# Two seven-product feed-forward stages: first-column products moved into the units in front, a new order of products, tiles and joins

## The chip, the core and the metric

The kernel runs on one core of a Trainium2 chip. The metric is the device time of one execution in microseconds. TensorE is PE in the profile, its weight loads PEld, VectorE DVE, ScalarE ACT, GpSimd POOL and SyncE SP; SP issues the DMA transfers of the stages that matter here.

## What is computed

Two transformer blocks on x of 1024 tokens by 1024 columns, all in float32. The two places that the change touches are the first halves of the two feed-forward layers, here called block 1's and block 2's up stage:

```python
h = rmsnorm(x, g_ffn[i])
x = x + jnp.square(jax.nn.relu(h @ w_ffn_up[i])) @ w_ffn_down[i]      # block 1: 1024 x 4096, 4096 x 1024
...
up = depthwise_conv(h @ w_up[l], conv_f_w[l], conv_f_b[l], FFN_CONV // 2)   # block 2: 1024 x 5632, three taps
act = jax.nn.gelu(up[..., :D_FF_2], approximate=True) * up[..., D_FF_2:]
x = x + act @ w_down[l]                                                # 2816 x 1024
```

## The kernel before

**Products.** A float32 matmul is three matmuls (`three`, L398 to L402): each operand is kept as a high part, rounded, and a low part, the rest. For a weight tile ACT writes the high part (`weight_hi`, L435) and POOL the low part behind it (`weight_lo`, L457). PE can start on the tile when both are there.

**Units.** An up stage goes in units of 256 output columns: 16 in block 1 (f=1), 22 in block 2 (f=2). A unit's weights are two column blocks, the activations two token halves by two column halves, and the four quarter results are made with seven products in place of eight. Each product is twelve matmuls of 128x512 (4 column pieces by three). In the order of before:

- P1 and P2 use the first-column tile, called F here, a plain weight tile `weight_hi<-stage` of 128x1024. P1 writes a PSUM bank, ACT copies it to `kept` (L2266), and P2 adds onto the same bank, so P2 waits for that copy.
- P6 and P7 use tile A (`sum23`), P5 and P4 tile B (half `sum1`, half plain), P3 tile C (`sum4`, 128x512). The sums are four DVE instructions of 128x512 for a unit (`dve_weight_sums`, L486 to L491).
- Joins on DVE: U2 = P6 + kept (L2291), U3 = P7 + kept (L2294), and an output from each of P5, P4 and P3 (L2307). P7 waits for U2, P4 for U3, P3 for P5's join, because they add onto or reuse those banks.
- Block 1 then does relu and square on ACT (L2273 to L2279) and stores the result. Block 2 runs the three taps: `act_conv` (ACT, L2167) and two DVE instructions of 128x1024 (L2175, L2176), then gelu (ACT, L2183) and the product with the other half (DVE, L2190).

The activations' quarters (T1, T2, T3, T4, B22 and so on) are split too: `T_hi` by ACT (L724), `T_lo` by DVE (L736) or by POOL (L744).

**The weight ring.** In these stages four weight slots go round. Step `released` in the order, behind the last product of a tile, frees the tile's slot and puts the split of the tile four further on in that place of ACT's, POOL's and (for sums) DVE's queue. Every engine works its queue in order. `P2`, `P7`, `P4` and `P3` are the last products of F, A, B and C:

```python
def released(self, n=1):
    for _ in range(n):
        self.back += 1
        s = self.slot_of[self.back - 1]
        ...
            self.slot(s)
```

**The seam.** At the start of a stage the norm of the token rows 4 to 7 still runs while PE works on P1 of the units 0 to 3 (EARLY = 4), then on their P2; then the units begin, each unit from the fifth on with its own P1 and P2 inside: P1, P6, P2, P7, P5, P4, P3. At the end the down stage takes over: it needs split activations (`act_hi`, `act_lo`, L2373 and L2382) and weight tiles of its own.

Of the kernel before, what the change touches and what calls it, by code (L numbers as in the profile page):

```python
# [14 lines left out]
P = 128  # L15
S = 1024
# [40 lines left out]
OUTS, EARLY = 4, 4  # L57
SUM_ROWS, LATE_ROWS, RAW_ROWS = (0, 1, 2), (3, 4), (6, 7)
SPILLED = {1: SUM_ROWS + LATE_ROWS, 2: SUM_ROWS + LATE_ROWS + RAW_ROWS}
# [666 lines left out]

def dve_split_lo(K, nid, name, t):
    if name not in LOW_BY_POOL:
# [10 lines left out]
def pool_split_lo(K, nid, name, t):  # L739
    if name in LOW_BY_POOL:  # L740
        g, S = K.g, K.S
        (hi, lo), raw = quarter(K, name, t)
        g.wait_ge(S.hT_hi, (nid, name, t))
        g.q.tensor_tensor(lo, raw, hi.bitcast(F32), ALU.subtract).then_inc(*S.hT_lo_pool.up((nid, name, t)))  # L744


LOW_BY_POOL = ("T4",)


def need_quarter(K, nid, name):  # L750
    t = NT // 2 - 1 if name in ("B11", "B21") else NT - 1
    K.pe.wait_ge(K.S.hT_hi, (nid, name, t))
    K.pe.wait_ge(K.S.hT_lo_pool if name in LOW_BY_POOL else K.S.hT_lo, (nid, name, t))

# [1401 lines left out]
def act_conv(K, u, part):  # L2156
# [87 lines left out]
def out_slot(u, name):  # L2244
    return u if name == "P2" and u < EARLY else OUTPUTS[name][0]


def out_before(u, name):

    if name == "P2" and u < EARLY:  # L2250
        return None
    if u == 0:
        return OUTPUTS[name][0], "P2"
    if name == "P2" and u == EARLY:
        return None
    return u - 1, name


def act_product(K, f, u, name):
# [22 lines left out]
def dve_product(K, f, u, name):  # L2282
# [29 lines left out]
def sp_product(K, f, u, name):  # L2312
# [18 lines left out]
def sp_x_back(K, f, t):  # L2331
# [9 lines left out]
    elif t in LATE_ROWS:  # L2341
        sp.wait_ge(S.mm, ("P4", f, last))
    else:
# [533 lines left out]
def lay_out(K):  # L2877
# [112 lines left out]
    K.kept = [put("kept", [P, HALF]) for _ in range(KEPT_ROWS)]  # L2990
# [133 lines left out]
class Order:  # L3124
# [30 lines left out]
    def take_unit(self, f, u, first, second, again):  # L3155

        w = len(self.tiles)
        if again:
            r1 = self.load(first, ("sums", (f, u)), w)
        else:  # L3160
            r1 = self.load_of[self.unit_tiles[f, u][0]][0]
            self.load_uses[r1].append(("sums", (f, u)))
            self.load_end[r1] = w
        r2 = self.load(second, ("sums", (f, u)), w)
        self.load_uses[r2].append(("low", w + 1))
        self.load_end[r2] = w + 1
        for part in (2, 3, 4):
            self.load_of.append((r1, r2))
            self.tiles.append((None, (P, 4 if part == 4 else ND, P)))
            self.sums_of.append((f, u, part))  # L3170
        self.unit_tiles[f, u] += (w, w + 1, w + 2)
# [421 lines left out]

def order_unit_up(o, f, norm):

    io, units = o.io, UNITS_UP[f]
# [476 lines left out]
```

## Time and profile before

| | |
|---|---|
| three runs | 3518.33, 3519.07, 3520.52 us (median 3519.07) |
| the profiled execution | 3518.79 us, its span 3517.5 us |
| granted clock of PE, mean | 0.984 of full speed |
| PE, PEld busy | 96%, 78% of the span |
| DVE, ACT, POOL busy | 57%, 40%, 36% |
| block 1's up stage in the trace | about 1187 to 1518 us |
| block 2's up stage in the trace | about 2788 to 3282 us |

The span is the stretch that the trace covers; 1.3 us of the profiled execution lie outside it. A window's row gives for each engine its busy time and in brackets how many instructions began there. A PE instruction's busy time overlaps that of the next one, so time lost on PE is better read from the distance between starts than from idle time alone.

### The profile page before, as it was taken

What the parts mean: (1) busy time and instruction counts of PE and PEld (TensorE: products, weight loads), DVE (VectorE), ACT (ScalarE), POOL (GpSimd) and SP (SyncE); (2) the same over time, 40 slices, a digit from 0 to 9 for tenths busy, and PEclk for the clock granted to TensorE, in tenths of its full rate; (3) what the DMA queues carried; (4) which work ended last, traced back from release to release, by engine and by line L of the source; (5) the groups of instructions that cost most, each with busy time, mean ns of one, the idle gap of its engine ahead of it and who ended that gap; (6) DMA issues with size and microseconds to landing.
All of it is one profiled execution on the core that took longest, in us unless ns stands there. A gap on an engine that the chain in (4) does not pass through costs nothing.

```text
span 3517.5 us, 48865 instructions
## 1 busy us (share of the span) xinstructions
PE 3371.2 (96%) x19926; PEld 2730.7 (78%) x19926; DVE 2012.0 (57%) x2693; ACT 1395.0 (40%) x2361; POOL 1268.9 (36%) x694
## 2 busy tenths in 40 slices
PE   7999999999999899999999899999999969999999
PEld 6788888887668778888887677777788757777787
DVE  3655747337754733345555539985554666666554
ACT  4443433344433544431114547771232424444212
POOL 3212122110033434454441126662453335555542
PEclk9999999999999999999999999999999989999999
DMA  5101101110046233342222322223565312222422
GB/s 153 40 24 44 48 25 46 41 45 7 1 147 206 90 105 109 108 170 96 96 96 96 109 68 81 81 81 106 177 205 176 102 60 79 83 78 102 144 101 85
DMA packets 312015, 326.57 MB, mean 93 GB/s; under 512 B 14117, under 2 KB 232673, under 8 KB 311792
## 3 DMA queue, kind: packets, MB, share of 16 engines
q1 hardware_dynamic: 297184, 289.17, 25.4%
q10 hardware_dynamic: 11520, 25.17, 1.9%
q0 software_dynamic: 3088, 9.10, 0.7%
q8 instruction: 159, 2.61, 0.3%
q14 instruction: 64, 0.52, 0.0%
HBM read 252.08 MB, written 71.30 MB: 92 GB/s over the span
## 4 chain that ended last, share of the span: by engine, by line


## 5 line engine op out<-in xcount | busy, mean ns | idle before, releaser
L457 POOL TENSOR_TENSOR weight_lo<-stage,weight_hi 128x1024 fp32r<-128x1024 f32 (+4 forms) x269 | 615.4, 2293 | 1094.9 <-ACT weight_hi L435 1066.4
L2432 DVE TENSOR_TENSOR x<-x,psum 128x512 f32<-128x512 f32 x416 | 283.4, 687 | 281.5 <-PE psum L402 265.2
L435 ACT ACTIVATE weight_hi<-stage 128x1024 fp32r<-128x1024 f32 (+4 forms) x329 | 299.9, 925 | 327.1 <-PE psum L402 282.8
L400 PE MATMUL psum<-hT_hi,weight_hi 128*128 128x512 f32 x1024 | 411.4, 402 | 3.7 <-ACT weight_hi L435 2.1
L401 PE MATMUL psum<-hT_lo,weight_hi 128*128 128x512 f32 x1024 | 401.0, 392 | 0.0
L402 PE MATMUL psum<-hT_hi,weight_lo 128*128 128x512 f32 x1024 | 400.8, 391 | 0.0
L400 PE MATMUL psum<-weight_hi,act_hi 128*128 128x512 f32 x864 | 337.8, 391 | 4.7 <-DVE raw L2307 3.3
L401 PE MATMUL psum<-weight_lo,act_hi 128*128 128x512 f32 x864 | 337.3, 390 | 0.0
L402 PE MATMUL psum<-weight_hi,act_lo 128*128 128x512 f32 x864 | 337.1, 390 | 0.0
L457 POOL TENSOR_TENSOR weight_lo<-sum,weight_hi 128x512 fp32r<-128x512 f32 (+1 forms) x114 | 209.7, 1848 | 212.0 <-ACT weight_hi L435 212.0
L400 PE MATMUL psum<-T_hi,weight_hi 128*128 128x512 f32 x608 | 244.6, 402 | 38.7 <-DVE U L2291 32.1
L401 PE MATMUL psum<-T_lo,weight_hi 128*128 128x512 f32 x608 | 242.7, 399 | 0.0
L402 PE MATMUL psum<-T_hi,weight_lo 128*128 128x512 f32 x608 | 242.3, 399 | 0.0
L400 PEld LDWEIGHTS psum<-hT_hi,weight_hi 128*128 128x128 f32 x1024 | 193.7, 189 | 53.7 <-issue 5.5
L401 PEld LDWEIGHTS psum<-hT_lo,weight_hi 128*128 128x128 f32 x1024 | 193.9, 189 | 42.9 <-issue 4.1
L402 PEld LDWEIGHTS psum<-hT_hi,weight_lo 128*128 128x128 f32 x1024 | 193.6, 189 | 41.2
L400 PEld LDWEIGHTS psum<-weight_hi,act_hi 128*128 128x128 f32 x864 | 162.9, 189 | 39.8 <-DVE raw L2307 3.7
L400 PE MATMUL psum<-B_hi,weight_hi 128*128 128x512 f32 x456 | 180.7, 396 | 9.2 <-ACT kept L2266 6.6
L402 PEld LDWEIGHTS psum<-weight_hi,act_lo 128*128 128x128 f32 x864 | 162.9, 189 | 33.9
L401 PEld LDWEIGHTS psum<-weight_lo,act_hi 128*128 128x128 f32 x864 | 162.9, 189 | 33.6
L2382 POOL TENSOR_TENSOR act_lo<-act_raw,act_hi 128x1024 fp32r<-128x1024 f32 x54 | 128.9, 2408 | 147.7 <-ACT act_hi L2373 147.7
L435 ACT ACTIVATE weight_hi<-sum 128x512 fp32r<-128x512 f32 (+1 forms) x114 | 87.8, 771 | 235.4 <-DVE sum L491 178.5
(416 smaller groups left out, 7164.6 us busy)
## 6 DMA issues: line engine op xcount, KB each, us to landing
stage<-in_w_in SPq DMA_DIRECT2D x64, 512.0 KB, 3.8
act_raw<-scratch_act SPq DMA_DIRECT2D x54, 512.0 KB, 5.2
stage<-in_w_up SPq DMA_DIRECT2D x48, 512.0 KB, 3.7
stage<-in_w_ffn_up SPq DMA_DIRECT2D x36, 512.0 KB, 4.1
scratch_gates<-gate ACTq DMA_DIRECT2D x64, 256.0 KB, 2.0
gs<-scratch_gates SPq DMA_DIRECT2D x64, 256.0 KB, 2.9
stage<-in_w_out SPq DMA_DIRECT2D x32, 512.0 KB, 4.5
scratch_act<-out SPq DMA_DIRECT2D x64, 256.0 KB, 2.5
```

The source lines that it names most:

```text
L400: q.matmul(out, stat[0], mov[0], start=first, stop=False, skip_group_check=onto)
L401: q.matmul(out, stat[0], mov[1], start=False, stop=False, skip_group_check=onto)
L402: return q.matmul(out, stat[1], mov[0], start=False, stop=final, skip_group_check=onto)
L435: a.q.activation(hi[:, part], src, ACT.Copy).then_inc(*S.w_hi.up(w))
L457: g.q.tensor_tensor(lo[:, part], src, hi[:, part].bitcast(F32), ALU.subtract).then_inc(*S.w_lo_pool.up(w))
L2382: g.q.tensor_tensor(lo, K.act_raw[i % 4][:, :], hi.bitcast(F32), ALU.subtract).then_inc(*S.act_lo.up((f, i)))
L2432: v.q.tensor_tensor(dst, dst, K.bank(key), ALU.add).then_inc(*S.x.up(("f", f, g, t, n)))
```

## The change

- P1 and P2 of the units 5 and up ("singles") no longer stand in their own unit. `unit_products` deals them out over the units in front, one behind P7 and the rest behind P3. In some units two are placed, in some one.
- A unit's own products go P6, P5, P7, P4, P3.
- Five units (EARLY = 5) have P1 and P2 in the seam. The fifth `kept` buffer lies in the place of row 5 of x, which is therefore stored away and brought back; the rows of the down stage are ordered anew.
- Tiles are taken in the order in which they are released; the first column block is loaded a second time for the sums of every unit, which adds 28 transfers of 512 KB (11 units in block 1, 17 in block 2).
- Joins stand apart from their products: those of P7 and P5 behind P7, taps begin with `conv_first` ahead of the join or the split.
- In the seam ten high splits of quarters stand behind P1 of unit 0 instead of two, and B22's low split for rows 4 and 5 goes to POOL.
- PSUM's ring of banks starts at bank 0 at the first down product.

```diff
-OUTS, EARLY = 4, 4
+OUTS, EARLY = 4, 5
 SUM_ROWS, LATE_ROWS, RAW_ROWS = (0, 1, 2), (3, 4), (6, 7)
-SPILLED = {1: SUM_ROWS + LATE_ROWS, 2: SUM_ROWS + LATE_ROWS + RAW_ROWS}
+KEPT_ROW = 5
+SPILLED = {1: SUM_ROWS + LATE_ROWS + (KEPT_ROW,), 2: SUM_ROWS + LATE_ROWS + (KEPT_ROW,) + RAW_ROWS}
...
+def low_by_pool(name, t):
+    return name == "T4" or (name == "B22" and t in POOL_LOW_ROWS)
...
+        elif u == KEPT_ROWS - 1:
+            a.wait_ge(S.spill[KEPT_ROW], f)
+            a.wait_ge(S.xn, (K.up_norm[f], KEPT_ROW))
...
-FIRST_ROWS = {1: (5, 6, 7, 0, 1, 2, 3, 4), 2: (5, 0, 1, 2, 3, 4, 6, 7)}
+FIRST_ROWS = {1: (6, 7, 0, 1, 2, 3, 4, 5), 2: (0, 1, 2, 3, 4, 5, 6, 7)}
...
+    if (g, t, n) == (0, FIRST_ROWS[f][0], 0):
+        K.ring_at["all"] = 0
...
+    def take_first(self, f, u, first):
+        self.unit_tiles[f, u] = (self.take(first),)
+
+    def take_part(self, f, u, part, first, second):
 
         w = len(self.tiles)
-        if again:
+        if part == 2:
...
+RELEASES = {"P2": 1, "P7": 2, "P4": 3, "P3": 4}
+
+
+def unit_products(f):
+
+    units = UNITS_UP[f]
+    singles = [(v, name) for v in range(EARLY, units) for name in ("P1", "P2")]
+    plan, done = [], 0
+    for u in range(units):
+        upto = min(len(singles), -(-u * len(singles) // (units - 2)))
+        more = singles[done:upto]
+        done = upto
+        plan.append([(u, "P6"), (u, "P5"), (u, "P7"), *more[:1], (u, "P4"), (u, "P3"), *more[1:]])
+    return plan
...
-    def block(u, i):
-        return weight_block(up, unit_blocks(f, u)[i] * P)
-
-    def first(u):
-        o.unit_tiles[f, u] = (o.take(block(u, 0)),)
-
-    def rest(u, again):
-        o.take_unit(f, u, block(u, 0), block(u, 1), again)
-    nid = {1: 2, 2: 5}[f]
-    for u in range(EARLY):
-        first(u)
-    for u in range(EARLY):
-        rest(u, True)
-    for u in range(EARLY, units):
-        first(u)
-        rest(u, False)
-
-    def product(u, name, back=1):
+    plan = unit_products(f)
+    early = [(u, name) for us in (range(EARLY - 1), range(EARLY - 1, EARLY)) for name in ("P1", "P2") for u in us]
+    for u, name in early + [p for unit in plan for p in unit]:
+        if name in RELEASES:
+            blocks = [weight_block(up, i * P) for i in unit_blocks(f, u)]
+            if name == "P2":
+                o.take_first(f, u, blocks[0])
+            else:
+                o.take_part(f, u, RELEASES[name], *blocks)
+
+    def product(u, name, join=True, back=True):
         o.do("product", f, u, name)
-        if name in ("P2", "P7", "P4", "P3"):
-            o.released(back)
+        if join:
+            o.do("join", f, u, name)
+        if back and name in RELEASES:
+            o.released()
...
     advance(norm, 2)
-    o.do("spill", f, LATE_ROWS[1])
-    if f == 2:
-        for t in RAW_ROWS:
-            o.do("spill", f, t)
+    for t in (LATE_ROWS[1], KEPT_ROW) + (RAW_ROWS if f == 2 else ()):
+        o.do("spill", f, t)
     product(0, "P1")
     advance(norm, 1)
-    high("T2", 4, 5)
+    for name in ("T2", "T4", "B22", "T1", "T3"):
+        high(name, 4, 5)
+    for name in ("T4", "B22"):
+        low(name, 4, 5)
     low("T2", 4, 5)
     o.released()
     product(1, "P1")
     advance(norm, 1)
-    high("T3", 4, 5)
-    low("T3", 4, 5)
+    low("T1", 4, 5)
     product(2, "P1")
     advance(norm, 1)
     finish(norm)
     if f == 2:
         o.do("raw_edges")
-    high("T2", 6, 7)
-    high("T3", 6, 7)
-    high("T4", 4, 5, 6, 7)
-    low("T4", 4, 5, 6, 7)
+    for name in ("T2", "T1", "T4", "T3", "B22"):
+        high(name, 6, 7)
+    low("T4", 6, 7)
     product(3, "P1")
     product(0, "P2")
     low("T2", 6, 7)
-    low("T3", 6, 7)
     product(1, "P2")
-    high("T1", 4, 5, 6, 7)
-    low("T1", 4, 5, 6, 7)
+    low("T1", 6, 7)
+    low("T3", 4, 5, 6, 7)
     product(2, "P2")
-    high("B22", 4, 5, 6, 7)
-    product(3, "P2", 0)
-    for u in range(units):
-        end = u == units - 1
-        for name in ("P1", "P6", "P2", "P7", "P5", "P4", "P3"):
-            if u >= EARLY or name not in ("P1", "P2"):
-                product(u, name)
-            if (u, name) == (0, "P6"):
+    if f == 2:
+        o.do("raw_first", 0)
+    product(3, "P2")
+    product(4, "P1")
+    product(4, "P2", back=False)
+    for u, unit in enumerate(plan):
+        for v, name in unit:
+            if v != u:
+                product(v, name)
+            elif name == "P6":
+                product(u, "P6", join=False)
+                if f == 2 and u:
+                    o.do("conv_first", u - 1, 0)
+                o.do("join", f, u, "P6")
+                if u == 0:
+                    o.released()
+                    low("B22", 6, 7)
+                if f == 2 and u:
+                    o.do("conv", u - 1, 0)
+                if u == last:
+                    for i in range(4):
+                        o.do("act_load", f, i)
+            elif name == "P5":
+                product(u, "P5", join=False)
+            elif name == "P7":
+                product(u, "P7", join=False, back=False)
+                if f == 2 and u:
+                    o.do("raw_first", u)
+                o.do("join", f, u, "P7")
+                o.do("join", f, u, "P5")
+                if f == 2 and u:
+                    o.do("gated", u - 1)
                 o.released()
-            if (u, name) == (0, "P7"):
-                low("B22", 4, 5, 6, 7)
-            if f == 2:
-                if u and name == "P6":
-                    o.do("gated", u - 1)
-                if name == "P2":
-                    o.do("raw_first", u)
-                if name in ("P4", "P3"):
-                    o.do("conv", u, 1 if name == "P4" else 0)
-            if end and name == "P1":
-                for i in range(4):
-                    o.do("act_load", f, i)
-            if end and name == "P7":
-                for i in range(2):
-                    o.do("act_split", f, i)
-                for t in SUM_ROWS[:2]:
-                    o.do("x_back", f, t)
+                if u == last:
+                    for i in range(2):
+                        o.do("act_split", f, i)
+                    for t in SUM_ROWS[:2]:
+                        o.do("x_back", f, t)
+            elif name == "P4":
+                product(u, "P4", back=False)
+                if f == 2:
+                    o.do("conv_first", u, 1)
+                o.released()
+                if f == 2:
+                    o.do("conv", u, 1)
+            else:
+                product(u, "P3")
     if f == 2:
-        o.do("gated", units - 1)
-    for t in SUM_ROWS[2:] + LATE_ROWS:
+        o.do("conv_first", last, 0)
+        o.do("conv", last, 0)
+        o.do("gated", last)
+    for t in SUM_ROWS[2:] + LATE_ROWS + (KEPT_ROW,) + (RAW_ROWS if f == 2 else ()):
         o.do("x_back", f, t)
-    if f == 2:
-        for t in RAW_ROWS:
-            o.do("x_back", f, t)
```

What this moves is seen in the order of the instructions on each engine. In the seam of block 1 ACT splits the high part of F of unit 3 (`weight_hi_59`) behind P1 of unit 0 (`kept_213` is its copy). `T_hi_199` is T2, `T_hi_203` T4, `B_hi_202` B22, `T_hi_200` T1 and `T_hi_201` T3. ACT before:

```order
L2266 ACTIVATE kept_213<-psum 128x512 [waits mm_done]
L724 ACTIVATE T_hi_199<-T_raw_204 128x4x128 [waits quarter_sum_ready] x2
L435 ACTIVATE weight_hi_59<-stage_53 128x1024 [waits stage_load1]
L2266 ACTIVATE kept_214<-psum 128x512 [waits mm_done]
L667 ACTIVATE B_raw_206<-psum 128x4x128 [waits mm_done]
L724 ACTIVATE T_hi_201<-T_raw_207 128x4x128
L724 ACTIVATE T_hi_201<-T_raw_207 128x4x128 [waits quarter_sum_ready]
```

ACT of the changed kernel, from the same copy on:

```order
L2277 ACTIVATE kept_213<-psum 128x512 [waits mm_done]
L725 ACTIVATE T_hi_199<-T_raw_204 128x4x128 [waits quarter_sum_ready] x2
L725 ACTIVATE T_hi_203<-T_raw_205 128x4x128 [waits spill_store4,spill_store3,xn_ready]
L725 ACTIVATE T_hi_203<-T_raw_205 128x4x128 [waits quarter_sum_pool_ready]
L725 ACTIVATE B_hi_202<-B_raw_206 128x4x128 [waits hT_raw_ready] x2
L725 ACTIVATE T_hi_200<-T_raw_208 128x4x128 x2
L725 ACTIVATE T_hi_201<-T_raw_207 128x4x128
L725 ACTIVATE T_hi_201<-T_raw_207 128x4x128 [waits quarter_sum_ready]
L436 ACTIVATE weight_hi_59<-stage_53 128x1024 [waits stage_load1]
```

Eight more high splits stand ahead of `weight_hi_59`.

On PE the place where a P1 begins whose tile is new, in the units of block 1. `B_hi_190` is the activation quarter of P1, `B_hi_202` that of P3, `T_hi_201` that of P7, and the number behind `weight_hi` is the slot. PE before, in the fifth unit:

```order
L401 MATMUL psum<-B_lo_196,weight_hi_59 128x512
L402 MATMUL psum<-B_hi_202,weight_lo_60 128x512
L400 MATMUL psum<-B_hi_190,weight_hi_61 128x512 [waits w_lo_pool_ready,w_hi_ready,act_op_done]
L401 MATMUL psum<-B_lo_191,weight_hi_61 128x512
L402 MATMUL psum<-B_hi_190,weight_lo_62 128x512
```

PE of the changed kernel, in unit 3, where P1 of unit 7 follows P7:

```order
L402 MATMUL psum<-T_lo_197,weight_hi_61 128x512
L403 MATMUL psum<-T_hi_201,weight_lo_62 128x512
L401 MATMUL psum<-B_hi_190,weight_hi_61 128x512 [waits w_lo_pool_ready,w_hi_ready,act_op_done]
L402 MATMUL psum<-B_lo_191,weight_hi_61 128x512
L403 MATMUL psum<-B_hi_190,weight_lo_62 128x512
```

P1 now has the slot (61) of the product directly ahead of it, so its tile can only be split once that product has ended. Counted over both stages, between the last product on a slot and the P1 that uses the slot next there stood four products in 28 of 30 places and five in two (the first tiles of the seam are not counted). Now it is none in 6 places (3 in each block), two in 11 (4 in block 1, 7 in block 2) and three in 13. P5's tile B had five or four ahead of it and has two in 6 places.

In block 2 the queues ahead of such a split. ACT before: gelu (L2183), then F (`weight_hi_57<-stage_54`), then the raw copy (L2152), A (`weight_hi_59`), B (`weight_hi_61`):

```order
L2266 ACTIVATE kept_213<-psum 128x512 [waits mm_done]
L2183 ACTIVATE xn_186<-xn_186 128x1024 [waits dve_op_done]
L435 ACTIVATE weight_hi_57<-stage_54 128x1024 [waits mm_done,stage_load2]
L2152 ACTIVATE raw_228<-psum 128x512
L435 ACTIVATE weight_hi_59<-sum_169_217 128x1024 [waits mm_done,weight_sums_ready]
L435 ACTIVATE weight_hi_61<-sum_170_218 128x512 [waits mm_done]
L435 ACTIVATE weight_hi_61<-stage_52 128x512
```

ACT of the changed kernel in a unit with two between: raw copy, gelu, A (`weight_hi_55<-sum_170`), F (`weight_hi_57<-stage_54`), and taps:

```order
L2179 ACTIVATE xn_186<-raw_229,param_50 128x1024 [waits act2_store,act_evac_done,products_joined]
L2164 ACTIVATE raw_229<-psum 128x512 [waits dve_op_done]
L2195 ACTIVATE xn_186<-xn_186 128x1024
L436 ACTIVATE weight_hi_55<-sum_170_218 128x1024 [waits mm_done,weight_sums_ready]
L436 ACTIVATE weight_hi_57<-stage_54 128x1024 [waits mm_done,stage_load2]
L2179 ACTIVATE xn_187<-raw_230,param_50 128x1024 [waits dve_op_done,products_joined]
```

DVE of the changed kernel there: U3 (L2305), P5's join (L2318), the gated product (L2202), and the four sums for which A waits:

```order
L2305 TENSOR_TENSOR U_174_222<-psum,kept_216 128x512 [waits mm_done]
L2318 TENSOR_TENSOR raw_230<-psum,U_174_222 128x512 [waits dve_op_done,products_joined]
L2202 TENSOR_TENSOR xn_186<-xn_186,xn_187 128x1024 [waits act_op_done]
L487 TENSOR_TENSOR sum_171_219<-stage_54 128x512 [waits w_lo_pool_ready,stage_load2,stage_load1]
L489 TENSOR_TENSOR sum_170_218<-sum_171_219,stage_53 128x512 [waits weight_sums_ready]
L490 TENSOR_TENSOR sum_170_218<-stage_53,stage_54 128x512
L492 TENSOR_TENSOR sum_172_220<-stage_53,sum_170_218 128x512 [waits weight_sums_ready]
```

F, which before was split ahead of A, now stands behind A, and A behind seven DVE instructions that begin with the end of P7.

## Rows read from the trace of the kernel before

**Rows 1.** The page, busy time of each engine over the span.

```profile
PE 3371.2 (96%) x19926; PEld 2730.7 (78%) x19926; DVE 2012.0 (57%) x2693; ACT 1395.0 (40%) x2361; POOL 1268.9 (36%) x694
```

**Rows 2.** Windows, block 1: stretch, length, busy of PE, PEld, DVE, ACT, POOL; clock, DMA, GB/s.

```profile
1212.00:1276.00 64.00, 51.67 (x195) 40.32 (x194) 34.06 (x39) 28.50 (x47) 28.78 (x18) 0.89 0.37 114
1276.00:1500.00 224.00, 224.00 (x986) 184.06 (x986) 83.07 (x107) 105.05 (x165) 100.77 (x59) 1.00 0.34 108
1500.00:1518.00 18.00, 16.94 (x76) 13.73 (x75) 3.46 (x5) 10.14 (x14) 12.17 (x7) 1.00 0.83 273
```

**Rows 3.** The same windows in block 2: seam, units, hand-over.

```profile
2812.00:2912.00 100.00, 70.92 (x266) 55.80 (x266) 63.46 (x64) 33.23 (x43) 39.37 (x22) 0.85 0.21 66
2912.00:3250.00 338.00, 331.45 (x1437) 266.84 (x1436) 229.02 (x240) 140.76 (x172) 179.87 (x85) 1.00 0.25 82
3250.00:3282.00 32.00, 28.38 (x111) 22.50 (x111) 17.11 (x17) 15.06 (x15) 22.93 (x9) 0.89 0.65 240
```

**Rows 4.** Waits of PE, 1198 to 1290: us in total, times, longest.

```profile
PE psum L400 <- DVE U L2291: 7.5, 4, 2.8
PE psum L400 <- issue: 3.3, 1, 3.3
```

**Rows 5.** Waits of PE, 2799 to 2925.

```profile
PE psum L400 <- DVE U L2291: 24.5, 4, 8.9
```

**Rows 6.** Waits of PE, 2925 to 3250.

```profile
PE psum L400 <- ACT kept L2266: 6.4, 17, 0.4
```

**Rows 7.** Windows, two stretches right behind a wait of PE.

```profile
1243.00:1246.40 3.40, 3.40 (x9) 2.64 (x9) 0.00 (x0) 0.00 (x0) 1.90 (x1) 0.50 0.49 139
...
2848.60:2854.10 5.50, 5.43 (x13) 4.27 (x14) 1.24 (x2) 0.99 (x2) 0.00 (x0) 0.50 0.24 95
```

**Rows 8.** Timeline of the seam of block 1: start, us, engine, instruction, idle before.

```profile
1193.04 1.04 ACT L435 ACTIVATE weight_hi<-stage 128x1024 fp32r<-128x1024 f32 x1
...
1194.16 3.23 POOL L457 TENSOR_TENSOR weight_lo<-stage,weight_hi 128x1024 fp32r<-128x1024 f32 x1 [3.00 <-ACT weight_hi L435]
...
1198.53 0.48 PE L400 MATMUL psum<-B_hi,weight_hi 128*128 128x512 f32 x1
```

**Rows 9.** Groups by form, 1186 to 1212: busy, mean ns of one, idle before.

```profile
L724 ACT ACTIVATE T_hi<-T_raw 128x512 fp32r<-128x512 f32 x12 | 6.7, 621 | 3.8 <-DVE T_raw L695 3.8
...
L744 POOL TENSOR_TENSOR T_lo<-T_raw,T_hi 128x512 fp32r<-128x512 f32 x4 | 6.7, 1698 | 0.9 <-ACT T_hi L724 0.9
```

**Rows 10.** Groups by form, the units of block 1.

```profile
L2279 ACT ACTIVATE out<-out 128x512 f32<-128x512 f32 x44 | 27.8, 632 | 1.4
...
L457 POOL TENSOR_TENSOR weight_lo<-stage,weight_hi 128x1024 fp32r<-128x1024 f32 x11 | 26.3, 2395 | 64.8 <-ACT weight_hi L435 64.8
...
L486 DVE TENSOR_TENSOR sum<-stage 128x512 f32<-128x512 f32 x11 | 20.9, 1903 | 0.0
...
L435 ACT ACTIVATE weight_hi<-stage 128x1024 fp32r<-128x1024 f32 x11 | 11.5, 1045 | 0.0
...
L2294 DVE TENSOR_TENSOR U<-psum,kept 128x512 f32<-128x512 f32 x11 | 7.6, 692 | 51.6 <-PE psum L402 51.6
...
L491 DVE TENSOR_TENSOR sum<-stage,sum 128x512 f32<-128x512 f32 x11 | 7.5, 683 | 0.0
```

**Rows 11.** Groups by form, the units of block 2.

```profile
L2176 DVE SCALAR_TENSOR_TENSOR xn<-raw,param,xn 128x1024 f32<-128x1024 f32 x34 | 59.2, 1741 | 1.2
...
L457 POOL TENSOR_TENSOR weight_lo<-stage,weight_hi 128x512 fp32r<-128x512 f32 x17 | 38.7, 2276 | 0.0
...
L2190 DVE TENSOR_TENSOR xn<-xn,xn 128x1024 f32<-128x1024 f32 x16 | 19.6, 1225 | 8.4 <-ACT xn L2183 8.4
```

**Rows 12.** Timeline of the hand-over of block 1.

```profile
1512.33 4.75 POOL L2382 TENSOR_TENSOR act_lo<-act_raw,act_hi 128x1024 fp32r<-128x1024 f32 x2
...
1517.22 0.47 PE L400 MATMUL psum<-weight_hi,act_hi 128*128 128x512 f32 x1 [1.06 <-POOL act_lo L2382]
```

**Rows 13.** Waits of PE, the hand-over of block 2.

```profile
PE psum L400 <- DVE raw L2307: 3.3, 1, 3.3
```

More of the change, by code:

```diff
@@ L739, in pool_split_lo @@
 def pool_split_lo(K, nid, name, t):
-    if name in LOW_BY_POOL:
+    if low_by_pool(name, t):
         g, S = K.g, K.S
@@ L743, in pool_split_lo @@
         g.wait_ge(S.hT_hi, (nid, name, t))
+        if name == "B22":
+            g.wait_ge(S.part, (nid, "T3", t))
         g.q.tensor_tensor(lo, raw, hi.bitcast(F32), ALU.subtract).then_inc(*S.hT_lo_pool.up((nid, name, t)))
-LOW_BY_POOL = ("T4",)
+POOL_LOW_ROWS = (4, 5)
 def need_quarter(K, nid, name):
@@ L2153, in act_raw_first, with act_conv_first @@
     K.free(key, S.act_evac)
-def act_conv(K, u, part):
+def act_conv_first(K, u, part):
     a, S, c = K.a, K.S, part * NF2 + u
@@ L2244, in out_slot, with act_join @@
 def out_slot(u, name):
-    return u if name == "P2" and u < EARLY else OUTPUTS[name][0]
+    return u if name == "P2" and u < OUTS else OUTPUTS[name][0]
 def out_before(u, name):
[L2250 to L2259, printed above, removed]
+    if name == "P2" and u <= OUTS:
+        return None if u < OUTS else (0, name)
+    return (OUTPUTS[name][0], "P2") if u == 0 else (u - 1, name)
+def act_join(K, f, u, name):
     a, S, key = K.a, K.S, ("unit", PRODUCTS[name][0], f, u)
@@ L2309, in dve_product, with sp_join @@
             K.free(key, S.joined)
-def sp_product(K, f, u, name):
+def sp_join(K, f, u, name):
     if f == 1 and name in OUTPUTS:
@@ L2342, in sp_x_back @@
         sp.wait_ge(S.mm, ("P4", f, last))
+    elif t == KEPT_ROW:
+        sp.wait_ge(S.joined, (f, last, "C21"))
     else:
@@ L2989, in lay_out @@
     m.lo = last_slot
-    K.kept = [put("kept", [P, HALF]) for _ in range(KEPT_ROWS)]
+    K.kept = [put("kept", [P, HALF]) for _ in range(KEPT_ROWS - 1)]
+    m.lo = x_at + KEPT_ROW * D * 4
+    K.kept.append(put("kept", [P, HALF]))
     m.lo = x_at
@@ L3153, in take @@
         return len(self.tiles) - len(tiles)
-    def take_unit(self, f, u, first, second, again):
+    def take_first(self, f, u, first):
+        self.unit_tiles[f, u] = (self.take(first),)
+    def take_part(self, f, u, part, first, second):
         w = len(self.tiles)
-        if again:
+        if part == 2:
             r1 = self.load(first, ("sums", (f, u)), w)
+            r2 = self.load(second, ("sums", (f, u)), w)
         else:
[L3161 to L3171, printed above, removed]
+            r1, r2 = self.load_of[self.unit_tiles[f, u][1]]
+        if part == 3:
+            self.load_uses[r2].append(("low", w))
+            self.load_end[r2] = w
+        self.load_of.append((r1, r2))
+        self.tiles.append((None, (P, 4 if part == 4 else ND, P)))
+        self.sums_of.append((f, u, part))
+        self.unit_tiles[f, u] += (w,)
     def used_upto(self):
@@ L3965, in scalar_program @@
             "output": act_output, "branch_load": act_branch_load, "gate_sum": act_gate_sum,
-            "merge_rows": act_merge_rows, "split_hi": act_split_hi, "product": act_product,
-            "act_split": act_act_split, "raw_first": act_raw_first, "conv": act_conv, "gated": act_gated, "down_rows": act_down_rows,
+            "merge_rows": act_merge_rows, "split_hi": act_split_hi, "join": act_join,
+            "act_split": act_act_split, "raw_first": act_raw_first, "conv_first": act_conv_first, "gated": act_gated, "down_rows": act_down_rows,
             "store_rows": act_store_rows, "ple_mix": act_ple_mix, "x2_stored": act_x2_stored, "rates": act_rates,
@@ L3987, in vector_program @@
             "branch_load": dve_branch_load, "gate_sum": dve_gate_sum,
-            "merge_rows": dve_merge_rows, "parts": dve_parts, "split_lo": dve_split_lo, "product": dve_product, "raw_edges": dve_raw_edges, "conv": dve_conv, "gated": dve_gated,
+            "merge_rows": dve_merge_rows, "parts": dve_parts, "split_lo": dve_split_lo, "join": dve_join, "raw_edges": dve_raw_edges, "conv": dve_conv, "gated": dve_gated,
             "down_rows": dve_down_rows, "store_rows": dve_store_rows, "p_turn": dve_p_turn, "ple_mix": dve_ple_mix,
@@ L4014, in sync_program @@
             "pair_load": sp_pair_load, "gate_load": sp_gate_load, "branch_fetch": sp_branch_fetch,
-            "gate_sum": sp_gate_sum, "residual": sp_residual, "spill": sp_spill, "product": sp_product, "x_back": sp_x_back,
+            "gate_sum": sp_gate_sum, "residual": sp_residual, "spill": sp_spill, "join": sp_join, "x_back": sp_x_back,
             "act_load": sp_act_load, "gated": sp_gated, "store_rows": sp_store_rows, "ple_load": sp_ple_load,
```

13 lines of the change are left out of this document (9 added, 4 removed).

## Prediction

> **What bounds the kernel now.** I read the page first: PE is busy for 96% of the span [rows 1], so only time in which PE stands or runs slowly can be won. The windows then say where the two up stages lose it. In the units of block 1 PE starts 986 matmuls in 224.00 us, which is 0.2272 us a matmul and 2.73 us a product of twelve, and hardly stops [rows 2]. I take 0.2272 us as the pitch and call everything above it lost. Length less count times pitch gives, in block 1, seam 64 - 195 x 0.2272 = 19.7, hand-over 18 - 76 x 0.2272 = 0.7 [rows 2]; in block 2, seam 100 - 266 x 0.2272 = 39.6, units 338 - 1437 x 0.2272 = 11.5, hand-over 32 - 111 x 0.2272 = 6.8 [rows 3]. Together 78.3 us. That is all that the change can win.
>
> The waits of PE name the causes. In block 1's seam they are four waits for U2 and one for the low part of the first A ("issue", 3.3) [rows 4]; in block 2's, four waits for U2, the longest 8.9, since U2 stands on DVE behind sums and taps [rows 5]. In block 2's units P2 waits 17 times for the `kept` copy [rows 6]; with the pipeline refilling, that is the 11.5 above. The rest of the seams' loss is the clock. Right behind a wait of 2.4 us the granted clock is 0.50 for 3.4 us, behind one of 8.4 us for 5.5 us [rows 7], half of 2.4 GHz. A stretch of 3.4 us at half speed costs 1.7 us, the longer one 2.75. I charge 1.7 for each new wait of over 2.5 us.
>
> The Trainium skill (TensorE: Matmul & The Clock Gate, "HAM oscillation") states that gaps in a stream of matmuls put the engine back to half rate, so that each gap is paid for again. By that rule, the trace agrees: 0.50 behind both.
>
> **What the change removes.** U2 gets P5 between P6 and P7, F's copies get a product in between, and seam units no longer queue four deep behind the sums. I let all 78.3 us go.
>
> **What it adds.** Let p be the end of a P7; PE could go on with the next product at p - 0.16, since starts overlap ends.
>
> *P1 directly behind P7 on the same slot, 6 places.* The tile can't be split before p. In block 1, ACT's queue has relu and square of P5's result first, and these wait for U3 and P5's join on DVE: 0.69 each, 1.3 with their overlap. Relu and square are 0.63 each (2.6), F's high part 1.05 (3.65), its low part 2.40 (6.05) [rows 10]. With the hand-overs between engines and the overlap, P1 stands 6.4 us. Three times (6.4 + 1.7) = 24.3. In block 2 there is no relu, and gelu stands ahead but mostly before p. High part 1.05 and low part 2.40 to 3.23 [rows 8, 10] give 3.5 to 4.9; I take 4.4. Three times (4.4 + 1.7) = 18.3.
>
> *P1 with two products ahead, 11 places.* F's split stands behind A's, and A's behind the four sums. Block 1, four places: joins 1.3, sums four times 0.68, 2.7 (4.0), A's high 1.05 (5.05), A's low 2.40 (7.45), F's low 2.40 (9.85) [rows 10]; PE is there at three products, 8.0. Stall 1.85, too short for me to charge the clock: 7.4. The first sum takes 1.90 us on average in block 1 [rows 10], which would make it 3.05 with a slow stretch behind it; I keep that as the upper end, 19. Block 2, seven places: joins 1.3, gated product 1.23 (2.5) [rows 11], sums 2.7 (5.2), A's high 1.05 (6.3), then two low splits of 2.40 to 3.23 each [rows 8, 10], ready at 11.1 to 12.7 against 8.0. I take the middle, 3.9, because the taps run on DVE beside the splits: they take 1.74 us on average there and half-width low splits 2.28 [rows 11]. Seven times (3.9 + 1.7) = 39.2.
>
> The Trainium skill (GPSIMD Engine Reference, "1. Specifications") states that POOL shares its SBUF interfaces with DVE and contends with DVE instructions of two SBUF inputs, as sums and taps are. The trace agrees, 3.23 us beside DVE's splits in the seam against a mean of 2.40 [rows 8, 10]; by the rule alone each stall of these seven would be the upper end, 4.7 us.
>
> *Tiles with less room in block 2.* In three units B has two products (5.5 us) from P4's end. The C21 join and `conv_first` go first (1.9 together), one half high (0.6), two halves low of 2.28 [rows 11]: 7.1, so 1.4 to 1.6 late. Where only a P2 is placed, A is late by some 0.8, three times. Together 6.6; both may be zero.
>
> *Seam, both blocks.* F of unit 3 has eight more high splits ahead (6.7 us for twelve, so 4.5) [rows 9] and on POOL four quarter splits, 1.70 each with DVE beside [rows 9]. Its high part began at 1193.04 and its low part ended at 1197.39, its P1 began at 1198.53 [rows 8]. The high part would end at about 1198.6; POOL, from 1194.2 on, needs 5.2 to 7.0 for its four and then 2.4 to 3.2 for the tile, so 1201.8 to 1204.4 and I take 1202.6. P1 is late by 4.1 us (3.2 to 5.8): twice (4.1 + 1.7) = 11.6. P2 of unit 4 stands directly behind its P1 and waits for a copy (0.8), P4 of the first and of the last unit directly behind P7 for U3 (0.95 each): 2.7 a stage, 5.4.
>
> *Hand-overs.* In block 1 the down stage's first product needs act_lo, POOL at 2.4 a piece [rows 12]. After p come joins, relu and square (2.6), a weight's high and low (6.05) and two act_lo (10.85), and only P4 and P3 are left to cover it, to 6.0: 4.85 + 1.7 = 6.6, where the wait was 1.06 [rows 12]. In block 2 the same without relu gives 4, a slow stretch 1.7, and the old wait of 3.3 for DVE behind the taps [rows 13] stays: 9.0.
>
> *At nothing:* 28 transfers of 512 KB. DMA is busy 0.34 and 0.25 of the units' windows [rows 2, 3], and 14.7 MB over 560 us is 26 GB/s beside 82 to 108. Uncovered, one landing late would cost some 4 us. The bank reset is held by the DVE wait in any case. The spill and return of row 5 lie beside products.
>
> Sum: 24.3 + 18.3 + 7.4 + 39.2 + 6.6 + 11.6 + 5.4 + 6.6 + 9.0 = 128.4. Less 78.3 it is +50.1 on the profiled execution's 3518.8, so **3569 us**; the runs' median is 0.3 us above that execution, which changes nothing.
>
> **Rivals.**
> - *Forecast, 0.58:* as above, 3545 to 3592, since the two sizes with the widest bounds (39.2 and 7.4) move it by some 12 each way and the clock by as much.
> - *Waits short, clock kept, 0.17.* New waits stand alone between full stretches, and if none is followed by half speed the sum loses 17 x 1.7 = 28.9; with POOL undisturbed it loses 3 x 0.9 + 7 x 0.8 = 8.3, and without the 6.6 it is 84.6: 3525. For it: in block 1's units all low splits ran at 2.40 [rows 10]. Against: [rows 7].
> - *Waits long, 0.14.* First sum at 1.90, two splits at 3.23, 2.75 of clock a time: 6.4 + 2.75 and 4.9 + 2.75 three times each (50.4), 19, seven times (4.7 + 2.75) = 52.2, 6.6, twice 8.5 (17), 5.4, 18: 168.6, so 3609.
> - *Faster or no change, 0.11: the sums' chain is shorter than I read it.* Its place is DVE's queue behind P7. If F's low part ended by p + 8.0, all eleven places and the 6.6 would cost nothing, 53.2 less: 3516. From there every wait followed by full speed (10 x 1.7) brings it to 3499. For it: DVE stands 51.6 us before U3 in block 1's units [rows 10], so it has time. Against: the order on DVE puts the sums behind U3 and P5's join, and then no idle time ahead of U3 helps. It decides the sign only if it is 1.9 us shorter in block 1 and 3.1 or more in block 2.
>
> **How the numbers follow.** A measurement of this kernel can tell 0.2%, 7 us, from no change. The forecast, the short and the long case lie above that, 0.89, less a part of the short one that ends within it (0.03): slower 0.86. The last rival splits into 0.07 faster and 0.04 same, so same is 0.07. The range takes in the short case and half of the long one: 3524 to 3600; it leaves out 0.11 below and some 0.07 above.
>
> **What the profile will show.** PE's waits in both up stages name POOL's `weight_lo` (or its issue), six of 4 to 6.5 us each directly behind P7, seven of 3 to 5 in block 2, with granted clock 0.50 behind them; the waits for U2 and `kept` are gone. P1 of unit 3 in each seam begins 4 us late. The units' windows fall below 1.00 in clock. I am wrong if F's low part in those places is there when P7 or P3 ends, or if PE's waits in the units add up to less than 30 us.

## The result

The changed kernel takes 3605.31 us (median of four runs, 3603.46 to 3606.92) against 3518.7 us before; the ratio is 1.0246, with a 95% interval of 1.0228 to 1.0264. It is 86.6 us slower. The forecast of slower holds, the size does not: 50 us were forecast, and the time lies 5 us above the range.

The page after, busy time by engine, against [rows 1]:

```profile
PE 3390.8 (94%) x19926; PEld 2746.3 (76%) x19926; DVE 2023.3 (56%) x2689; ACT 1388.8 (39%) x2361; POOL 1275.9 (35%) x698
```
Windows of the changed kernel (columns as in [rows 2]): the stretch that was block 1's seam, a piece behind a wait of a unit, the units of block 2, and a piece behind another wait:

```profile
1212.00:1276.00 64.00, 62.44 (x275) 51.11 (x274) 32.71 (x38) 31.28 (x50) 30.82 (x17) 1.00 0.44 134
1294.40:1298.20 3.80, 3.80 (x9) 3.03 (x10) 0.00 (x0) 0.00 (x0) 0.00 (x0) 0.50 0.02 4
2912.00:3340.00 428.00, 363.15 (x1480) 290.74 (x1478) 267.44 (x257) 142.17 (x177) 187.73 (x91) 0.93 0.28 86
2981.60:2987.80 6.20, 6.16 (x15) 4.85 (x16) 1.58 (x2) 0.66 (x2) 4.59 (x3) 0.50 0.22 65
```
From 1212 us on the seam is full where before it was empty in many places: 275 matmuls begin in 64 us against 195 [rows 2]. (One wait of this seam lies ahead of the window and is shown below.) The loss has gone into the units, which in block 1 had none: block 2's window has 1480 starts in 428 us, and 1480 x 0.2272 is 336. The second and fourth rows are work at half speed, 9 starts in 3.8 us and 15 in 6.2 us.

The waits of PE in the units of block 1 (1290 to 1545 us), then of block 2 (2915 to 3335 us), each in us in total, times, longest:

```profile
PE psum L401 <- POOL weight_lo L458: 20.2, 6, 6.3
PE psum L401 <- ACT out L2288: 7.5, 4, 1.9
```
```profile
PE psum L401 <- POOL weight_lo L458: 60.6, 19, 7.5
PE psum L401 <- DVE U L2302: 4.1, 3, 1.5
```
In block 1's units PE waited for nothing before, in block 2's for `kept` alone [rows 6]. Now it is POOL's low split nearly everywhere. The row "ACT out" is the four places with two products between: F's low part ends there within 0.1 us of one of ACT's relus (in the first at 1323.31, the relu at 1323.35), and the profile names the later one.

The first place where P1 stands directly behind P7 in block 1 (unit 3; timeline: start, us, engine, instruction). P7 ends at 1288.05, P1 begins at 1294.34:

```profile
1288.09 0.69 DVE L2305 TENSOR_TENSOR U<-psum,kept 128x512 f32<-128x512 f32 x1 [3.30 <-PE psum L403]
1288.81 0.69 DVE L2318 TENSOR_TENSOR out<-psum,U 128x512 f32<-128x512 f32 x1
1289.54 0.63 ACT L2288 ACTIVATE out<-out 128x512 f32<-128x512 f32 x1 [4.25 <-DVE out L2318]
1290.20 0.63 ACT L2290 ACTIVATE out<-out 128x512 f32<-128x512 f32 x1
1290.73 1.04 ACT L436 ACTIVATE weight_hi<-stage 128x1024 fp32r<-128x1024 f32 x1
1291.85 2.34 POOL L458 TENSOR_TENSOR weight_lo<-stage,weight_hi 128x1024 fp32r<-128x1024 f32 x1 [4.09 <-ACT weight_hi L436]
```
Joins, relu, square, high part, low part, one behind the other, as summed in the prediction: PE stands 6.45 us beyond its pitch, 6.4 were forecast. The same place in block 2 (unit 4). P7 ends at 2941.68, P1 begins at 2949.16:

```profile
2940.27 2.38 DVE L2187 SCALAR_TENSOR_TENSOR xn<-raw,param,xn 128x1024 f32<-128x1024 f32 x1 [1.66 <-ACT xn L2179]
2942.69 1.28 DVE L2188 SCALAR_TENSOR_TENSOR xn<-raw,param,xn 128x1024 f32<-128x1024 f32 x1
...
2944.01 0.60 ACT L2164 ACTIVATE raw<-psum 128x512 f32<-128x512 f32 x1 [3.77 <-DVE xn L2188]
2944.51 1.05 ACT L2195 ACTIVATE xn<-xn 128x1024 f32<-128x1024 f32 x1
2945.45 1.05 ACT L436 ACTIVATE weight_hi<-stage 128x1024 fp32r<-128x1024 f32 x1
2946.58 2.43 POOL L458 TENSOR_TENSOR weight_lo<-stage,weight_hi 128x1024 fp32r<-128x1024 f32 x1 [5.00 <-ACT weight_hi L436]
```
Here ACT's raw copy (L2164) waits until DVE has finished the taps at 2943.97, 2.3 us after P7's end. Gelu stands behind the copy, F's high part behind gelu, and the low part ends at 2949.01. PE stands 7.6 us, not 4.4. And a place of block 2 with two products between. P7 ends at 2969.53. The P2 behind it, the last product on the slot, ends at 2972.25, then come P4 and P3, and P1 begins at 2981.64, 4.1 us late, where 3.9 were forecast:

```profile
2969.57 0.69 DVE L2305 TENSOR_TENSOR U<-psum,kept 128x512 f32<-128x512 f32 x1 [2.23 <-PE psum L403]
2970.29 0.69 DVE L2318 TENSOR_TENSOR raw<-psum,U 128x512 f32<-128x512 f32 x1
2970.90 1.21 DVE L2202 TENSOR_TENSOR xn<-xn,xn 128x1024 f32<-128x1024 f32 x1
2972.03 0.68 DVE L487 TENSOR_TENSOR sum<-stage 128x512 f32<-128x512 f32 x1
...
2973.96 0.68 DVE L492 TENSOR_TENSOR sum<-stage,sum 128x512 f32<-128x512 f32 x1
2974.68 1.06 ACT L436 ACTIVATE weight_hi<-sum 128x1024 fp32r<-128x1024 f32 x1 [5.77 <-DVE sum L492]
2975.65 1.04 ACT L436 ACTIVATE weight_hi<-stage 128x1024 fp32r<-128x1024 f32 x1
2975.82 2.40 POOL L458 TENSOR_TENSOR weight_lo<-sum,weight_hi 128x1024 fp32r<-128x1024 f32 x1 [10.89 <-ACT weight_hi L436]
2978.17 3.33 POOL L458 TENSOR_TENSOR weight_lo<-stage,weight_hi 128x1024 fp32r<-128x1024 f32 x1
...
2979.33 3.25 DVE L2188 SCALAR_TENSOR_TENSOR xn<-raw,param,xn 128x1024 f32<-128x1024 f32 x1
```
The joins and the gated product begin with P7's end, and the sums run from 2972.03 to 2974.65. Then come A's high part, F's high part, A's low part (2.40) and F's low part, which takes 3.33 us with the taps on DVE beside it, against 2.34 and 2.43 above. The tap beside it takes 3.25 us, against 1.28 at 2942.69. The Trainium skill (GPSIMD Engine Reference, "1. Specifications") has POOL and DVE share their SBUF interfaces, with contention where a DVE instruction has two SBUF inputs, as the taps have; the trace agrees, by these numbers. P1 of unit 3 in the seam of block 1 began late too, by 4.4 us beyond its pitch where 4.1 were forecast:

```profile
1204.45 0.76 PE L401 MATMUL psum<-B_hi,weight_hi 128*128 128x512 f32 x1 [4.34 <-POOL weight_lo L458]
```
The hand-over of block 2, against [rows 13]: the wait for DVE is still there, now 4.1 us at the ninth product, and one for act_lo has come.

```profile
PE psum L401 <- DVE x L2447: 4.1, 1, 4.1
PE psum L401 <- POOL act_lo L2395: 3.4, 1, 3.4
```

### The profile page after: what moved, and what is told of

Read it like the earlier page. It is cut to its first block, busy times and chain, and to the rows that moved or that the text cites. A ratio compares the mean times of both kernels' runs of the same rounds, so it can differ in the third digit from the quotient of the medians.

```text
span 3605.6 us, 48830 instructions
## 1 busy us (share of the span) xinstructions
PE 3390.8 (94%) x19926; PEld 2746.3 (76%) x19926; DVE 2023.3 (56%) x2689; ACT 1388.8 (39%) x2361; POOL 1275.9 (35%) x698
## 4 chain that ended last, share of the span: by engine, by line
## 5 line engine op out<-in xcount | busy, mean ns | idle before, releaser
L401 PE MATMUL psum<-B_hi,weight_hi 128*128 128x512 f32 x456 | 193.8, 425 | 87.9 <-POOL weight_lo L458 77.7
L401 PE MATMUL psum<-T_hi,weight_hi 128*128 128x512 f32 x608 | 239.7, 394 | 19.6 <-POOL weight_lo L458 12.2
L402 PE MATMUL psum<-B_lo,weight_hi 128*128 128x512 f32 x456 | 190.3, 417 | 0.0
L403 PE MATMUL psum<-B_hi,weight_lo 128*128 128x512 f32 x456 | 189.7, 416 | 0.0
```

The costliest lines, as they stand in the source:

```text
L401: q.matmul(out, stat[0], mov[0], start=first, stop=False, skip_group_check=onto)
L402: q.matmul(out, stat[0], mov[1], start=False, stop=False, skip_group_check=onto)
L403: return q.matmul(out, stat[1], mov[0], start=False, stop=final, skip_group_check=onto)
```

## The experiments

All of them are edits of the changed kernel, but for e5, and none leaves work out. A wait's length in the rows is idle time; the text mostly gives the distance between starts beyond the pitch, which is some 0.16 us more.

**e1: deal out pairs.** In `unit_products`:

```diff
-        upto = min(len(singles), -(-u * len(singles) // (units - 2)))
+        upto = 2 * min(units - EARLY, -(-u * (units - EARLY) // (units - 2)))
```

> The changed kernel with one thing different: P1 and P2 of a unit are dealt out as a pair, both into the same unit in front or none, so that no tile has fewer than three products between the last use of its slot and its own first use (before: none in 6 places, two in 11). Products, joins, loads, seam and hand-over are those of the changed kernel, and so are the 28 additional transfers. Theory (distance on the slot): the waits of PE for POOL's weight_lo in the units go, and with them 19.4 + 8.1 us of waits in block 1, 22.9 + 28.8 in block 2, the tile B waits of 6.5 and about 32 us of half clock: 3605 - 118 = about 3487, up to 3505 if units without a pair wait for DVE. Rival A (additional transfers or splits beside DVE are too slow, wherever a single stands): stays above 3590. Rival B (the new order P6, P5, P7 itself costs): some 3550.

3498.16 us (3495.54 to 3501.74), 107 us less than the changed kernel, and 0.9946 of the time before (0.9931 to 0.9961). What PE still waits for in block 2's units:

```profile
PE psum L401 <- DVE U L2305: 9.6, 4, 2.9
PE psum L401 <- DVE U L2302: 3.8, 3, 1.5
PE psum L401 <- ACT raw L2164: 1.3, 3, 0.5
PE psum L401 <- POOL weight_lo L458: 0.4, 1, 0.4
```
The longest wait for POOL left in the units is 0.4 us, with the same loads, the same splits and the same order within a unit. The edit also brings tile B back from two products between to three or more. Rival A is out, and rival B too. What has come up are waits for U2 and U3 in the units that have no pair: there P6, P5, P7, P4, P3 follow each other and DVE is behind. The four U3 waits (9.6 us) contain three of 2.9. The sum of the theory was 118 us less those; 107 came.

**e2: the seam.** The split of unit 3's tile goes ahead of the added quarters:

```diff
-    for name in ("T2", "T4", "B22", "T1", "T3"):
-        high(name, 4, 5)
-    for name in ("T4", "B22"):
-        low(name, 4, 5)
+    high("T2", 4, 5)
     low("T2", 4, 5)
     o.released()
+    for name in ("T4", "B22", "T1", "T3"):
+        high(name, 4, 5)
+    for name in ("T4", "B22"):
+        low(name, 4, 5)
     product(1, "P1")
```

> The changed kernel with the eight added high splits and four low splits of quarters in the seam put behind the split of unit 3's first-column tile, as far as the changed kernel allows. Theory: P1 of unit 3 in both seams no longer waits 4.4 us and the half clock behind it (some 3.2 us a seam) goes: 3605 - 15 = 3590. Rival (the wait only moves, since the quarters' splits are late for P6 instead): within 4 us of 3605.

3603.09 us (3601.07 to 3604.65), 2 us less. In the seam of block 1:

```profile
PE psum L401 <- ACT kept L2277: 2.1, 2, 1.3
PE psum L401 <- POOL weight_lo L458: 1.8, 1, 1.8
```
The wait of P1 of unit 3 is gone, and two others have come behind it: 1.3 us for a `kept` copy at P2 of unit 3 and 1.8 us for the tile at P1 of unit 4. (The other `kept` wait, 0.7 us at P2 of unit 4, was there before.) In block 2's seam, 2812 to 2880 us, more waiting came back than went:

```profile
PE psum L401 <- ACT raw L2164: 3.7, 1, 3.7
PE psum L401 <- ACT kept L2277: 2.0, 2, 1.3
```
The rival is right for the most part. The cause of the wait was as said, its removal was not worth it: the seam's work on ACT and POOL is the same and only changes places.

**e3: block 2's queues.** Raw copy, gelu and gated product of all units go behind the split:

```diff
-                if f == 2 and u:
-                    o.do("raw_first", u)
                 o.do("join", f, u, "P7")
                 o.do("join", f, u, "P5")
-                if f == 2 and u:
-                    o.do("gated", u - 1)
                 o.released()
+                if f == 2 and u:
+                    o.do("raw_first", u)
+                    o.do("gated", u - 1)
```

> The changed kernel with, in block 2, the raw copy, gelu and gated product of the unit before put behind the split released by P7 instead of ahead of it. Theory (in the three places where P1 stands directly behind P7, ACT holds F's split back behind the raw copy, which waits for taps on DVE): 7.64 us there become about 3.8, and in the seven places with two products between the sums start 1.2 us sooner, 4.1 becomes 2.9: 11.5 + 8.4 = 20 us and perhaps some half clock, 3605 - 20 = 3585. Rival (the slot alone sets it, or taps on DVE hold back the joins too): less than 5 us.

3613.77 us (3609.04 to 3616.27), 8 us more.

```profile
PE psum L401 <- POOL weight_lo L458: 45.9, 20, 4.6
PE psum L401 <- ACT raw L2164: 16.8, 3, 5.6
PE psum L401 <- DVE U L2302: 8.5, 6, 1.7
```
The waits for POOL fell from 7.6 to 4.8 us (three places) and from 4.1 to 3.0 (seven places), much as the theory has it. But the raw copy frees a PSUM bank, and in three units P1 of a unit four further on needs that bank: three new waits of 5.6 us. The waits for U2 grew as well, from 4.1 us to 8.5. I had left out who waits for what I moved. e11 does it without them.

**e11: the same in three units alone**, where a P1 follows P7 on the same slot in block 2 (`gated` moves as `raw_first` does):

```diff
+                single = f == 2 and [name for v, name in unit if v != u] == ["P1"]
-                if f == 2 and u:
+                if f == 2 and u and not single:
                     o.do("raw_first", u)
                 ...
                 o.released()
+                if single:
+                    o.do("raw_first", u)
+                    o.do("gated", u - 1)
```

> The changed kernel with raw copy, gelu and gated product put behind the split released by P7 only in the three units of block 2 in which P1 of a later unit stands directly behind P7. Theory: ACT held F's high part back behind a raw copy that waited for taps on DVE; without it the high part begins at P7's end, and the low part runs beside the taps (3.25 instead of 2.43), so 7.64 becomes about 4.8, three times, as in e3, without what e3 added elsewhere: 3605 - 8.6 = 3596, or down to 3591 with less half clock. Rival (the forecast's reading: the slot and the two splits set it, the copy does not matter): 3605.

3598.03 us (3594.29 to 3599.36), 7 us less. Around the first of the three places:

```profile
PE psum L401 <- POOL weight_lo L458: 6.1, 2, 4.7
```
The longest is 4.7 us where it was 7.5. What stood ahead of F's high part on ACT, left out of the forecast, is so shown to have held it back. Raw copy and gelu moved together; that 2.3 us of the 3.8 were the copy's wait for the taps and the rest the two instructions themselves is read from the rows above, not shown by a run of its own. The gain is smaller than 3.8, since the low part now runs beside the taps.

**e9: block 1's queue.** P5's join, and with it relu and square, behind the split, in block 1 alone:

```diff
-                o.do("join", f, u, "P5")
+                if f == 2:
+                    o.do("join", f, u, "P5")
                 ...
                 o.released()
+                if f == 1:
+                    o.do("join", f, u, "P5")
```

> The changed kernel with P5's join, and with it relu and square of its result, put behind the split released by P7, in block 1 alone. Theory (the wait is the chain from P7's end through ACT's queue): where P1 stands directly behind P7, F's high part begins at P7's end instead of 2.7 us later and the three waits of 6.45 us become 3.7; with two products between, the sums start 0.6 us sooner, 2.0 becomes 1.4 in four places; P3 then waits some 0.6 us for P5's join in the units without a product between P7 and P4. Sum -8.2 - 2.4 + 3, with less half clock behind the three: 3605 - 8 to -12 = 3595. Rival (reuse of the slot costs a fixed time, however the queues stand): 3605.

3595.31 us (3594.65 to 3598.83), 10 us less. All waits of PE of more than a pitch from 1280 to 1520 us:

```profile
PE psum L401 <- POOL weight_lo L458: 20.7, 10, 3.7
```
The longest, the three behind P7, are now 3.9 us beyond the pitch, from 6.45. The four with two products between did not fall as expected (2.0 became 2.2); why is open. The fixed-time rival is out: the wait is the queue ahead of the split, then the split.

**e4: the hand-over.** The first two activation splits of the last unit go ahead of the weight tile's split, in place of behind it:

```diff
+                if u == last:
+                    for i in range(2):
+                        o.do("act_split", f, i)
                 o.released()
                 if u == last:
-                    for i in range(2):
-                        o.do("act_split", f, i)
                     for t in SUM_ROWS[:2]:
```

> The changed kernel with the first two activation splits of each down stage put ahead of the weight tile's split that P7 of the last unit releases. Theory: the first down product waits for the second act_lo, which stands on POOL behind a weight's low part that is needed only eight products later; 3.4 us of the 4.6 and of the 3.6 us wait go, and the half clock behind them (2.4 and 1.7): 3605 - 7 to 11 = 3594 to 3598. Rival (the loads of the activations are the limit): no change.

3603.31 us (3602.03 to 3606.69), no more than 2 us less. In block 1 the wait of 4.6 us became 2.9. In block 2:

```profile
PE psum L401 <- DVE x L2447: 6.2, 1, 6.2
PE psum L401 <- POOL act_lo L2395: 3.6, 1, 3.6
```
act_lo is late still (3.6 us), because ACT's first high part there waits for the activation's load, and the wait for DVE has grown to 6.2 us. The theory holds in part in block 1, where 1.8 us of the wait went and not 3.4, and the rival holds in block 2.

**e5: the bank alone, on the kernel before.** In `pe_down`:

```diff
+    if (g, t, n) == (0, FIRST_ROWS[f][0], 0):
+        K.ring_at["all"] = 0
     b = K.open(key)
```

> The kernel before with one line of the change: PSUM's ring of banks starts at bank 0 at the first down product of each down stage. Theory: the wait of 3.3 us at the hand-over of block 2 is for DVE, which is behind the taps whatever bank is next; the ninth product of the down stage waits about as long instead: 3518, within 2 us. Rival (the bank alone is the cause): the 3.3 us and the half clock behind them go, 3518 - 5 = 3513.

3515.23 us (3512.4 to 3520.91), ratio 0.9996 (0.9987 to 1.0005).

```profile
PE psum L400 <- DVE x L2434: 5.6, 1, 5.6
```
The wait of 3.3 us [rows 13] is gone at its place and one of 5.6 us stands later, for DVE's `x` additions. The bank is worth nothing that stands clear of the scatter, and by the trace the wait has only moved.

**e6, e7, e8, e10: from e1 on.** e6 has four units in the seam with five kept buffers, so that one unit more in each block has a pair. e7 is e1 with e4's edit in block 1 alone. e8 is e7 with taps and raw copy behind the joins in units without a pair. e10 puts e6, e2's seam and e7 together. The edits of e6 and e8:

```diff
-OUTS, EARLY = 4, 5
+OUTS, EARLY = 4, 4
-KEPT_ROWS = EARLY
+KEPT_ROWS = EARLY + 1
...
-    product(3, "P2")
-    product(4, "P1")
-    product(4, "P2", back=False)
+    product(3, "P2", back=False)
```

```diff
-                if f == 2 and u:
+                if f == 2 and u and len(unit) > 5:
                     o.do("conv", u - 1, 0)
...
-                if f == 2 and u:
+                if f == 2 and u and len(unit) > 5:
                     o.do("raw_first", u)
...
                 o.do("join", f, u, "P5")
+                if f == 2 and u and len(unit) == 5:
+                    o.do("conv", u - 1, 0)
+                    o.do("raw_first", u)
```

> e1 with four units instead of five in the seam (five kept buffers stay), so that 12 and 18 pairs are dealt out and one unit fewer in each block has no pair. Theory: in block 2 each unit without a pair costs some 6.4 us (U2 late 1.7, U3 late 3.1, half clock 1.7), in block 1 0.9, and P2 of unit 4 no longer waits right behind its P1 (0.8 each): 3498 - 9 = 3489. Rival (the seam needs the fifth unit as cover for the quarters' low splits): up to 5.4 us a seam lost again, 3500.

> e1 with the first two activation splits ahead of the released weight split in block 1 alone, where e4 showed the wait of 4.6 us shortened to 2.9, and not in block 2, where e4 showed it held by the activations' loads. Expected: 3498 - 3 = 3495.

> e7 with, in block 2's units without a pair alone, the first taps (two DVE instructions) and the raw copy put behind U3 and P5's join. Theory: in such a unit P4 waits 3.1 us for U3 because U3 stands on DVE behind the taps; with that gone three units lose 3.1 and the half clock 1.7 to 3.4: 3495 - 12 = 3483. Rival (the taps then hold back the sums and with them the next unit's A by as much): 3495 or more.

> e6 with the seam of e2 and the hand-over of e7 in block 1: pairs, four units in the seam, unit 3's tile split first, activation splits first. Theory: the gains add where they lie in different places: 3486 - 2.5 (hand-over) - 2 to 6 (two seams, where the 4.4 us wait and its half clock go but shorter waits on the P2 products come) = 3478 to 3482. Rival (with four units the seam has no cover for the later quarters' splits): 3486 or above.

e6 takes 3485.93 us (3483.37 to 3486.33), ratio to before 0.9907 (0.9893 to 0.9922), 12 us less than e1 where 9 were expected. e7 takes 3495.57 us (3493.61 to 3497.76), as expected within 1 us, but 2.6 us are about what the runs scatter. e8 takes 3496.0 us (3493.92 to 3497.61), nothing gained; its waits in block 2's units against those of e1 above:

```profile
PE psum L401 <- DVE U L2302: 8.8, 6, 1.7
PE psum L401 <- DVE U L2305: 3.1, 4, 0.8
```
U3's wait fell from 9.6 to 3.1 us and U2's rose from 3.8 to 8.8: what came off the one wait came onto the other, both for DVE. The rival's time is right; its place is not, since PE waits for U2 and not for tile A. e10 takes 3480.33 us (3474.66 to 3480.75), ratio 0.9889 (0.9874 to 0.9904), 38 us less than the kernel before. It still waits in block 2:

```profile
PE psum L401 <- DVE U L2305: 8.1, 4, 3.0
PE psum L401 <- POOL act_lo L2395: 4.1, 1, 4.1
PE psum L401 <- DVE U L2302: 3.6, 3, 1.5
```
## Why the forecast missed

By its own steps, from the distance between starts in the trace of the changed kernel (wait beyond the pitch, without the clock):

| term | forecast us | measured us |
|---|---|---|
| P1 behind P7, block 1, 3 places | 19.2 | 19.3 |
| P1 behind P7, block 2, 3 places | 13.2 | 22.9 |
| two products between, block 1, 4 | 7.4 | 8.1 |
| two products between, block 2, 7 | 27.3 | 28.8 |
| tiles B, A and U2 with less room | 6.6 | 19.9 |
| seam, P1 of unit 3, both blocks | 8.2 | 8.8 |
| seam and last unit, short waits | 5.4 | 5.7 |
| hand-overs | 12.2 | 12.5 |
| half clock | 28.9 | 42 |
| sum | 128.4 | 168 |

Less the 78.3 us that went, 168 gives +89.7; the profiled executions differ by 88.1. So the ledger closes within 2 us, and three of its terms were too small.

*The half clock* is the largest, 13 us. 17 stretches were charged at 1.7 us, 19 came at a mean of 2.2. "I charge 1.7 for each new wait of over 2.5 us" took the 3.4 us of [rows 7] for the rule and the 5.5 us for an exception. In the changed kernel 19 stretches at 0.50 lie in the two stages, 13 of them of 6.8 us, and in the worst case nearly all of it falls on work: behind the wait shown for block 2 PE resumed at 2981.64 and ran at half speed to 2987.8, 15 starts in 6.2 us, which costs 6.2 - 15 x 0.2272 = 2.8 us. The two rows were both on the table; I took the cheaper one.

*P1 behind P7 in block 2* is 9.7 us. The step that failed is "gelu stands ahead but mostly before p". I followed ACT's queue and not what its instructions wait for: the raw copy waits for taps on DVE, and these were late, since they stand behind the sums and U2. F's high part began at 2945.45, 3.8 us after P7's end, where the forecast had it begin at once. e11 and e3 show it: with copy and gelu behind the split, 7.6 us became 4.8.

*The tiles and U2*, 13 us, is the step "Together 6.6". Its three B waits of 1.6 and three A waits of 0.8 are there as forecast. Left out were block 1's B tiles (three of 0.6) and, in block 2, waits of 0.3 to 1.7 us, six of them 1.25 us or more: three for U2, which the forecast had as gone, and three for B, in the units behind those where only a P2 is placed.

What held: that all 78.3 us would go and come back elsewhere, the places (6 and 11), the chains of block 1 within 0.2 us, the seven waits with their contended low split (3.33 beside taps, the row of 3.23 [rows 8] was the right one to bound it by), DMA at nothing (e1 keeps all the added transfers and is faster than before), the bank at nothing (e5). The rival "waits long" named 3609 by other parts: 4.9 for what was 7.6, and 2.75 of clock each time for what was 2.2; that it came within 4 us is luck. The added transfers are 30 and not 28, by the traces' issues of `in_w_ffn_up` (48 against 36) and `in_w_up` (66 against 48), which changes nothing in the argument. The range was built as if the terms could miss independently; here all three misses had one sign, and all three are queues that were read a step too short.

The cause of the loss is settled by e1: it is the line that deals single products by count, where this ring of four slots needs three products between the last use of a slot and the first use of its next tile. With pairs the other parts of the change are worth 19 us, and 38 with e10's three more edits. What in e10 each of its edits brings alone is open, except for e6's.

## What to carry to other kernels

When a plan deals work out by a fraction, list for each buffer how many steps lie between its release and its next use, over all places: the minimum decides, not the mean. A wait in a dense stream of matmuls costs more than its length: here 2.2 us more on average over the 19 stretches at half clock, 2.8 in the case worked out above. Before an instruction is moved behind another, ask for each engine what it frees; a queue must be followed through the waits of its instructions, not only through their durations.

## What was not expected of the hardware

In the two up stages the stretches at half clock came in two lengths only, 3.4 and 6.8 us, in this trace and in those of e1, e3 and e9. The kernel before had two of 10.2 us there as well, around the waits of 8.4 and 8.9 us for U2. Of the four waits of 2.0 us in block 1 three were followed by none and one by a stretch of 3.4 us; the seven waits of 4.1 us in block 2 were followed by either length, with the same work around them.
